# Block two's up projection: one level of Strassen's algorithm in 512 columns against two levels in 256 columns

## What is computed

```python
def conv_glu_ffn(h, w_up, conv_w, conv_b, w_down):
    gate, val = jnp.split(h @ w_up, 2, axis=-1)
    gate = causal_dwconv(gate, conv_w, conv_b)
    return (jax.nn.silu(gate) * val) @ w_down
```

## Time and profile before

| | us |
|---|---|
| median of three runs | 4015.4 (4013.1 to 4016.0) |
| span of the profiled execution | 4018.9 |
| its stretch from the first up product to the first down product | 534.5 |

### The profile page before, as it was taken

One profiled execution on the slowest core, in us unless ns is written; L12 is line 12 of the kernel. 1 busy time (PEld: TensorE's weight loads), 2 busy tenths in 40 slices (PEclk: granted clock), 3 DMA queues, 4 the chain that ended last, 5 costly groups with the idle time before them and its releaser, 6 DMA issues. The chain is left out here.

```text
span 4018.9 us, 41721 instructions
## 1 busy us (share of the span) xinstructions
PE 3777.2 (94%) x16132; PEld 1727.8 (43%) x16132; DVE 2642.6 (66%) x3525; ACT 906.7 (23%) x1740; POOL 567.5 (14%) x415
## 2 busy tenths in 40 slices
PE   7999986999998999995999999899988999999998
PEld 3444442333333444442333333444476444444443
DVE  6878857888885787866788888355543343334676
ACT  2254321111112224421211111242342100000000
POOL 1000002121211000002112111000120022222541
PEclk8999997999999999997999999999999999999999
DMA  8210447999996601065899998311011111111454
GB/s 309 77 42 1 147 153 293 346 355 351 350 346 204 228 0 43 0 231 204 316 354 349 355 346 304 94 36 32 12 45 52 55 42 42 42 42 44 181 199 167
DMA packets 186966, 682.51 MB, mean 170 GB/s; under 512 B 16657, under 2 KB 80785, under 8 KB 137617
## 3 DMA queue, kind: packets, MB, share of 16 engines
q1 hardware_dynamic: 177264, 646.27, 43.0%
q0 software_dynamic: 9504, 33.56, 3.4%
HBM read 637.83 MB, written 41.94 MB: 169 GB/s over the span
## 5 line engine op out<-in xcount | busy, mean ns | idle before, releaser
L1751 PE MATMUL ps<-w_raw,h_act 128*64 128x512 f32 x2048 | 455.2, 597 | 6.2 <-ACT h_act L1865 6.2
L1804 PE MATMUL ps<-w_down,h_act 128*128 128x512 f32 x960 | 417.2, 592 | 0.6 <-DVE h_act L1986 0.6
L1751 PE MATMUL ps<-w_t,h_act 128*64 128x512 f32 x1536 | 342.0, 594 | 0.0
L3479 PE MATMUL ps<-h_act,arena_two 128*128 128x512 f32 x704 | 313.2, 592 | 1.8 <-ACT h_act L462 1.0
L1000 DVE SCALAR_TENSOR_TENSOR y<-y,par_one 128x1024 f32<-128x1024 f32 x240 | 307.4, 1281 | 3.1
L1751 PEld LDWEIGHTS ps<-w_raw,h_act 128*64 128x64 f32 x2048 | 148.7, 138 | 299.6 <-issue 299.6
L1804 PEld LDWEIGHTS ps<-w_down,h_act 128*128 128x128 f32 x960 | 180.1, 190 | 217.6 <-issue 215.2
L1727 POOL DMA_INDIRECT x_rows<-h_act,idx x30 | 161.0, 5367 | 569.6 <-DVE h_act L2031 569.6
L3479 PE MATMUL ps<-arena_two 128*128 128x512 f32 x528 | 237.3, 592 | 0.0
L2321 PE MATMUL ps<-h_act,arena_two 128*128 128x512 f32 x544 | 235.1, 592 | 1.1 <-DVE h_act L473 1.0
L660 PE MATMUL ps<-h_act,arena_a 128*128 128x512 f32 x512 | 223.3, 596 | 9.8 <-ACT h_act L462 5.0
(11 more groups left out here) (490 smaller groups left out, 5826.4 us busy)
## 6 DMA issues: line engine op xcount, KB each, us to landing
w_raw<-in_w_gate SPq DMA_DIRECT2D x128, 1024.0 KB, 7.0
w_raw<-in_w_up SPq DMA_DIRECT2D x128, 1024.0 KB, 9.5
w_down<-in_w_down SPq DMA_DIRECT2D x128, 1024.0 KB, 8.2
arena_two<-in_ffn_w_down SPq DMA_DIRECT2D x44, 1024.0 KB, 4.8
arena_two<-in_ffn_w_up SPq DMA_DIRECT2D x22, 1024.0 KB, 5.0
arena_b<-in_w_ada SPq DMA_DIRECT2D x32, 512.0 KB, 5.2
arena_two<-in_w_in SPq DMA_DIRECT2D x21, 512.0 KB, 4.0
arena_two<-x_rows SPq DMA_DIRECT2D x20, 512.0 KB, 7.0
```

The lines of the kernel that those rows point to most:

```text
L1751: last = nc.tensor.matmul(out[w * TOK:(w + 1) * TOK, :], left[:, k, :], right[:, w, k, :], start=begins and k == 0, stop=k == KH1 - 1, ski ...
L1804: last = nc.tensor.matmul(ps[:, 4 + i, :], hidT[:, k * P:(k + 1) * P], down[:, c, k % 2, i * HALF:(i + 1) * HALF], start=(k == 0), stop=(k ...
L3479: last = nc.tensor.matmul(ps[:, q % 8, :], left[:, k, :], right[k], start=k == 0, stop=k == KH - 1)
```

## The change

The up projection becomes 11 sets of two gate and two value tiles together. An outer level of Strassen's algorithm makes seven products of (512 x 256 weights) by (512 x 512 of h), and each of these is made by an inner level: seven products of two matmuls of 128 x 128 weights by 256 columns. Here q = 7n + i numbers the outer products, i in the order A11, A12, S2, S3, S1, S4, A22. An outer product is 28 instructions, a set 196. All 77 outer products are 2156 instructions.

- VectorE makes the outer sums of weights (`outer_left`, four of 128 x 1024 a set), three corner sums of every outer product (128 x 256, out of PSUM), and seven joins of whole products a set (128 x 1024). In the first set it also makes, between products, the outer sums of h and 28 inner ones (`inner_rights`).
- GpSimd makes four inner sums of weights for each outer product (`left_sums`, 128 x 256), in two buffers.
- ScalarE copies four quarters out of PSUM for each outer product. Four of the seven inner products of an outer one add up in one bank (`in_z`).
- The gated tiles no longer fit beside this: they go to DRAM (`store_hid`, 512 KB a tile), and each down round reads its own 2.75 MB back (`load_hid`, `load_hid_last`; two buffers, the next round's load is issued behind chunk 4's weights). The last set's tiles are stored behind the down weights 0 to 2 and ahead of the others.
- Product 0 runs ahead of the second half of the turning, with a wait on the last row of the mixer's output.

```diff
--- before.py
+++ after.py
...
+    def result(q):
+        return (z.u2, z.p_even, z.p_odd, z.u3, z.u4, z.p_even, z.p_odd)[q % 7]
+    def left_operand(q):
+        n, i = divmod(q, 7)
+        return (z.a11, z.a12, z.s2, z.a21, z.s1, z.s4, z.a22[n % 2])[i]
...
+            else:
+                engine.wait_ge(outer_s, 4 * n + {IN_S1: 1, IN_S2: 2, IN_S3: 3, IN_S4: 4}[i])
...
+                def store_hid(n):
+                    for i in range(2):
+                        sp.wait_ge(hid_made, 2 * n + i + 1)
+                        sp.dma_start(hid_rows[:, :, 2 * n + i, :].rearrange("r p t -> p r t"),
+                                     val[:, i, :].rearrange("p (r t) -> p r t", r=n_rounds)).then_inc(hid_stored, 16)
...
+                def load_hid(r):
...
+                    sp.dma_start(h[:, :, i * HALF:(i + 1) * HALF], hid_rows[r, :, 0:2 * KD, :].rearrange("p (k j) t -> p k (j t)", k=KD)).then_inc(hid_in[i], 16)
...
+                last_set = 7 * (n_sets - 1)
+                for n in range(n_sets):
+                    if n:
+                        store_hid(n - 1)
+                    if n + 1 < n_sets:
+                        load_21(n + 1)
+                        load_11(n + 1)
+                        load_12(n + 1)
+                        if n + 2 < n_sets:
+                            load_22(n + 2)
+                sp.wait_ge(m4_done, last_set + IN_A12 + 1)
                 down(0)
-                sp.wait_ge(tapped, CONV_FF * KF)
+                sp.wait_ge(hid_stored, 32 * (n_sets - 1))
+                load_hid(0)
+                sp.wait_ge(m4_done, last_set + IN_S2 + 1)
                 down(1)
-                sp.wait_ge(m4_done, n_sets)
                 down(2)
+                sp.dma_start(last_gain, a["norm_final"].partition_broadcast(P)).then_inc(row_loaded, 16)
+                sp.wait_ge(outer_s, 4 * n_sets)
                 again(0)
-                sp.dma_start(last_gain, a["norm_final"].partition_broadcast(P)).then_inc(row_loaded, 16)
+                store_hid(n_sets - 1)
+                sp.wait_ge(hid_stored, 32 * n_sets)
+                load_hid_last(0)
+                sp.wait_ge(m4_done, n_products)
                 again(1)
                 for q in range(n_ring, n_rounds * n_chunks):
                     wait_chunk(sp, q - n_ring)
                     down(q)
...
+                    if c == 4 and r + 1 < n_rounds:
+                        load_hid(r + 1)
+                        load_hid_last(r + 1)
...
+                def left_sums(q):
+                    x11, x12, x21, x22 = inner_blocks(left_operand(q))
+                    to = z.left_sums[q % 2]
+                    wait_left(pool, q)
+                    if q >= 2:
+                        pool.wait_ge(m7_done, q - 1)
+                    nc.gpsimd.tensor_tensor(to[:, 0], x21, x22, ALU.add).then_inc(left_made, 1)
+                    pool.wait_ge(left_made, 4 * q + 1)
+                    nc.gpsimd.tensor_tensor(to[:, 1], to[:, 0], x11, ALU.subtract).then_inc(left_made, 1)
+                    nc.gpsimd.tensor_tensor(to[:, 2], x11, x21, ALU.subtract).then_inc(left_made, 1)
+                    pool.wait_ge(left_made, 4 * q + 2)
+                    nc.gpsimd.tensor_tensor(to[:, 3], x12, to[:, 1], ALU.subtract).then_inc(left_made, 1)
+                for q in range(n_products):
+                    left_sums(q)
...
+                def m1(q):
+                    x11, _, _, _, _, _, _, y11, *_ = operands(q)
+                    wait_left(pe, q)
+                    outer_right(q, M1)
+                    if q >= 3:
+                        pe.wait_ge(c21_kept, q - 2)
+                    block_product(in_z(q), x11, y11, True).then_inc(m1_done, 1)
...
+                def m4(q):
+                    _, _, x22, *_, t4 = operands(q)
+                    pe.wait_ge(right_made, 4 * min(q, 6) + 4)
+                    pe.wait_ge(c22_made, q + 1)
+                    block_product(in_z(q), x22, t4, False).then_inc(m4_done, 1)
...
+                def product(q):
+                    m1(q)
+                    m5(q)
+                    m2(q)
+                    m6(q)
+                    if q:
+                        m4(q - 1)
+                    m3(q)
+                    m7(q)
...
                 pe.wait_ge(weighed, QT)
+                product(0)
                 turn(1)
                 pe.wait_ge(kept_act, 8)
                 pe.wait_ge(kept_dve, 8)
-                m1(1)
-                pe.wait_ge(kept_act, 8)
-                pe.wait_ge(kept_dve, 8)
-                for n in range(n_sets):
-                    if n >= 2:
-                        m1(n)
-                    if n:
-                        m2(n)
-                    m6(n)
-                    m7(n)
-                    m5(n)
-                    m3(n)
-                    m4(n)
-                done = (m1_done, m2_done, m6_done, m7_done, m5_done, m3_done, m4_done)
+                for q in range(1, n_products):
+                    product(q)
+                m4(n_products - 1)
...
+                for q in range(1, n_products):
+                    n, i = divmod(q, 7)
+                    keep_m1(q)
+                    keep_m5(q)
+                    keep_u2(q)
+                    keep_c21(q - 1)
+                    if n and i in (2, 3):
+                        silu(n - 1, i - 2)
+                keep_c21(n_products - 1)
+                for i in range(2):
+                    silu(n_sets - 1, i)
+                act.wait_ge(joined, 7 * n_sets)
...
+                def inner_rights(i):
+                    y11, y12, y21, y22, t1, t2, t3, t4 = z.rights[i]
+                    nc.vector.tensor_tensor(t1, y12, y11, ALU.subtract).then_inc(right_made, 1)
+                    dve.wait_ge(right_made, 4 * i + 1)
+                    nc.vector.tensor_tensor(t2, y22, t1, ALU.subtract).then_inc(right_made, 1)
+                    nc.vector.tensor_tensor(t3, y22, y12, ALU.subtract).then_inc(right_made, 1)
+                    dve.wait_ge(right_made, 4 * i + 2)
+                    nc.vector.tensor_tensor(t4, y21, t2, ALU.subtract).then_inc(right_made, 1)
+                def outer(made, to, left, right, part):
+                    ks = slice(2 * part, 2 * part + 2)
+                    nc.vector.tensor_tensor(to[:, ks], left[:, ks], right[:, ks], ALU.subtract).then_inc(made, 1)
...
+                def corner_22(q):
+                    dve.wait_ge(m5_kept, q + 1)
+                    dve.wait_ge(m7_done, q + 1)
+                    c = result(q)[:, 1, late]
+                    nc.vector.tensor_tensor(c, c, in_z(q), ALU.add).then_inc(c22_made, 1)
...
+                def join_product(q):
+                    n, i = divmod(q, 7)
+                    have = 7 * n
+                    whole(q)
+                    if i == 1:
+                        if n:
+                            dve.wait_ge(tapped, 2 * CONV_FF * n)
+                        join(have + 1, g[:, :, edge:edge + HALF], z.u2, z.p_even)
+                    elif i == 2:
+                        join(have + 2, z.u2, z.u2, z.p_odd)
+                    elif i == 3:
+                        join(have + 3, z.u3, z.u2, z.u3)
+                    elif i == 4:
+                        if n:
+                            dve.wait_ge(hid_stored, 32 * n)
+                        join(have + 4, val[:, :, second], z.u3, z.u4)
+                        join(have + 5, z.u4, z.u2, z.u4)
+                    elif i == 5:
+                        join(have + 6, g[:, :, edge + HALF:], z.u4, z.p_even)
+                    elif i == 6:
+                        join(have + 7, val[:, :, first_half], z.u3, z.p_odd)
...
+                    else:
+                        dve.wait_ge(a12_in, 16 * (n + 1))
+                        dve.wait_ge(outer_s, 4 * n + 2)
+                        if n:
+                            dve.wait_ge(m4_done, 7 * (n - 1) + IN_S4 + 1)
+                        nc.vector.tensor_tensor(z.s4, z.a12, z.s2, ALU.subtract).then_inc(outer_s, 1)
...
+                dve.wait_ge(kept_act, 4)
+                dve.wait_ge(kept_dve, 4)
+                inner_rights(IN_A11)
                 scale_row(core, dve, x, QT - 1, n_rows[QT - 1], rooted, inverted, normed)
+                inner_rights(IN_A12)
+                corner_11(0)
+                corner_12(0)
+                corner_22(0)
                 keep_half_dve(core, dve, 1, banks[1], shift_at, turned, kept_dve)
                 dve.wait_ge(kept_act, 8)
                 dve.wait_ge(kept_dve, 8)
+                outer(outer_t1, z.t1, z.b12, z.b11, 0)
+                dve.wait_ge(outer_t1, 1)
+                outer(outer_t2, z.t2, z.b22, z.t1, 0)
+                outer(outer_t1, z.t1, z.b12, z.b11, 1)
+                dve.wait_ge(outer_t1, 2)
+                outer(outer_t2, z.t2, z.b22, z.t1, 1)
+                dve.wait_ge(outer_t2, 2)
+                corner_11(1)
+                outer_left(0, 1)
+                outer_left(0, 2)
```

(78 more changed lines are left out.)

553 lines of the change are left out of this document (311 added, 242 removed), and 6 rows, old and new, of the table last_gain.

## The result

The changed kernel takes 4042.4 us (median of four, 4041.3 to 4044.7), the kernel before 4014.2 in the same comparison; ratio 1.0067, 95% interval 1.0055 to 1.0079. It is slower, and by more than 0.2%. Forecast were 4032 and +16.7; measured, the medians lie 28.2 apart. The profiled execution has a span of 4040.4.

What follows compares the result with a forecast made beforehand. TensorE's own stream was taken as the bound. Up stretch: 465.7 + 3.5 + 20 + 33 + 2.5 + 1 + 12 = 537.7 against 534.5; with 13.5 for the hand over, 16.7 us slower, median 4032, range 4003 to 4050.

Steps and rivals of the forecast that it cites:

- The stream: Up projection: 2156 TensorE instructions 0.216 us apart take 465.7 us, 62.8 less than before, with other engines' work mostly hidden underneath.
- the rival of loads outside: All 2156 instructions: weight loads of 0.19 us do not overlap matmuls, 410 us more, 4440; chance 0.01.
- Product 0 of a set: Join and two outer sums delay corner 22 for the next product's m4: 0.25 x 10 = 2.5 us.
- S4's stall: At product 5 of sets 1 to 10, TensorE waits 3.3 us for the fourth outer weight sum: 33 us.
- The falls of the clock in the sets: TensorE's clock drops behind two in three of the ten waits for S4's sum: 10 us.
- The first set, waits: TensorE waits for VectorE between the first set's products: 18.2 us, 20 with differences lengthened by GpSimd.
- The first set, clock: Time lost to TensorE's low clock in the first set: a flat 2 us.
- The hand over: Start of the down projection: late weight sums and down weights cost 10.5 us, plus 3 for two clock falls.
- that the clock holds: Rival: no clock falls over the 3.3 us stalls for S4's sum; 15 us go, 4017; chance 0.22.
- that the hand over is covered: Rival at the start of the down projection: reload and stores hide, 13.5 us less, 4019; chance 0.07.
- VectorE as the bound: Rival in the sets: VectorE, waiting for GpSimd sums, needs 44.2 of 42.3 us; 4047 in the middle; chance 0.14.
- S4 without a stall: Rival at product 5: the fourth outer weight sum is ready in time, so the kernel is faster, 3989; chance 0.08.

Runs made afterwards that it cites:

- The filled sets: Sets 1 to 9 of the changed kernel with six spare matmuls ahead of the wait for S4's sum; 4032.4 us, ratio 1.0036.
- s4_early: Changed kernel with the fourth outer sum of weights (S4) moved from behind product 4 to behind product 2; 4007.6 us, ratio 0.9975.
- s4_swap: Changed kernel with S4's outer sum placed ahead of the weighing instead of behind it; 4036.2 us, ratio 1.0053.
- fill_start: Changed kernel with spare matmuls in five of TensorE's waits in the first set; 4039.1 us by table last row 4040.6 us, ratio 1.0049.
- sp_order: Changed kernel with SyncE issuing down(3) and down(4) ahead of the last tiles' store, its wait and the reload; 4037.8 us, ratio 1.0049.
- handover: Changed kernel with down(3) and down(4) issued earlier, and VectorE's weight sums of chunks 2 and 3 made earlier; 4035.6 us, ratio 1.0046.
- no_inner: Changed kernel with VectorE computing only 8 of 256 columns of the first set's 28 inner differences; 4038.2 us, ratio 1.0057.
- s3_late: Changed kernel with S4's sum behind product 2 and S3's sum moved behind corner 22 of product 0; 3995.8 us, ratio 0.9947.

## Why the prediction was right, and where a term was off

Direction and range held; the forecast was 11.5 us short (+16.7 for +28.2). By its own steps:

- **The stream** (465.7) and its cover: right. The filled sets and the price of a period bear it out: 45.78 is 42.34 + 3.16 + 0.28. There is no gap between 256-column instructions; the rival of loads outside is out.
- **Product 0 of a set**: forecast 0.25 x 10. There is no wait there in the changed kernel: TensorE loses 0.04 us at that m4. The 0.28 above looks like this term and is another: nearly all of it stands around S4's stall, as the matmul ahead runs out and the first ones behind start late. I had nothing for that, at any wait. The lateness of corner 22 itself was real, hidden by the stall: s4_early shows it, 0.5 to 1.4.
- **S4's stall**: forecast 3.3 x 10, measured 3.16 x 10, at the place named and with GpSimd standing there. Shown by s4_early and s4_swap, which take out all of it and the weighing's share.
- **The falls of the clock in the sets**: forecast two in three at 1.5, 10 us; measured 8 at 1.68, 13.4. The longest row, 3.01 us, was the right neighbour.
- **The first set, waits**: forecast 18.2 to 20. Measured 18.9, with the 0.95 that was there before. The sum is right in part by luck: the 1.4 in the turning is not there, product 2 has 1.9 for 2.4, product 3 has 5.3 for 3.6, product 5 has 4.6 for 3.1.
- **The first set, clock**: this is the term that was mis-sized. I wrote "and 2 for the first set". The clock was low for 20.5 us of it, and 9.2 us were lost. It is most of the 11.8 by which product 7 was later than the forecast's 63.3; 2.0 stand around the waits, and 0.7 are longer waits. I had priced the ten stalls of the sets by rows and gave the first set, with five waits of 1.5 to 4.6 us close together, a flat figure. fill_start shows the size: waits the same, clock held, 7.3 us of 75.1 gone.
- **Last product**: 1.08, forecast 1.
- **The hand over**: 10.5 and 3 forecast; measured 3.34 + 4.16 + 1.42 = 8.9 of waits and one fall of 1.7, of the 12.4 by which that part is longer; 0.6 more stand behind the last matmul, and the other 1.2 I did not trace. (My working was loose: its own terms add up to 7.7 to 14.1, not 9.6 to 12.) Its two causes are as described: sp_order shows SyncE's, handover VectorE's. `down(5)` cost 1.4 and not 2 to 3.

In sum, the up stretch was 10.8 longer than forecast (548.5 for 537.7): 7.2 more for the clock of the first set, 3.4 more for that of the others, 5.0 around the waits (2.0 in the first set, 2.8 at the ten stalls, 0.2 at the last product), less 1.1 for the first set's waits, 1.4 for the stalls and 2.5 for product 0, are 10.6 of it. The part behind was 1.1 shorter than forecast (12.4 for 13.5). Together 9.7: the tail's +26.3 against +16.7. The 2 us between the tail and the medians lie within what the part ahead varies by.

The rivals: that the clock holds is refuted by eight falls; that the hand over is covered, by 12.4 us. VectorE as the bound had a real mechanism, but not its size. I had held that the rows show a partial loss, 0.16 on average. no_inner's row shows an instruction of 0.17 that stands until GpSimd's ends. That is the rule of the Trainium skill ("SBUF — State Buffer", "SBUF: two separate sides"), and here the trace agrees with it: 0.71 for 0.17. The mean of a group hides what one meeting costs: the 44 sums of L3690 take 0.68 to 0.95, the median is 0.94, so most of them lose 0.26, beside GpSimd's short sums of 128 columns. In the ordinary sets the loss fell mostly on GpSimd: in nine sets of the changed kernel 72 of its 252 sums of 0.73 take 1.6 or 1.7. VectorE's corners, weighings and sums of S2 to S4 keep their lengths; S1's sum, 10 of 63 joins and most taps do not. VectorE's lengths add up to 34.3 us a set, where I had 32.5 without a meeting and the rival 44.2, so there it did not decide. In s4_early, where the ten stalls are gone, it is short at product 0, and s3_late shows that 1.2 us moved out of the way are enough.

S4 without a stall was the rival at 3989, "faster", chance 0.08; it was not so in this kernel. As an edit it gave 4007.6 alone and 3995.8 with S3's sum moved: I had priced the gain without the wait that the stall had hidden.
